# A hybrid decoder step on one core: weight sums of a seven-product matrix block done by accumulating transfers

## The reference

```python
a, b = split(rmsnorm(x) @ w_in, 2)
x = x + 0.5 * (silu(a) * b) @ w_out
```

## Time and profile before

| what | value |
|---|---|
| median of 3 runs | 2186.99 us (2185.7 to 2189.09) |
| the profiled execution | 2188.33 us, span 2186.6 us |
| mean granted TensorE clock | 0.995 of full speed |
| busy: PE, DVE, ACT, POOL | 98%, 73%, 41%, 0% of the span |
| the DMA queues: SP's, POOL's | 35.5%, 0.3% of 16 engines' span |
| chain of work that ended last | PE 93%, DVE 5%; seven-product blocks (L2631) 33% |

### The profile page before, as it was taken

One profiled execution on the slowest core, in us unless ns is written; L12 is line 12 of the kernel. 1 busy time (PEld: TensorE's weight loads), 2 busy tenths in 40 slices (PEclk: granted clock), 3 DMA queues, 4 the chain that ended last, 5 costly groups with the idle time before them and its releaser, 6 DMA issues.

```text
span 2186.6 us, 42987 instructions
## 1 busy us (share of the span) xinstructions
PE 2142.7 (98%) x17360; PEld 2108.6 (96%) x17360; DVE 1600.6 (73%) x2462; ACT 906.9 (41%) x1284; POOL 5.7 (0%) x19
## 2 busy tenths in 40 slices
PE   9999999999999989999999999999989999999998
PEld 8999999999999889999999999999988999999998
DVE  5766776457878789778487887848797579686774
ACT  5222232234545455445155543515533345253443
POOL 0000000000000000000000000000000000000000
PEclk9999999999999999999999999999999999999999
DMA  5233543243242144445245242424374434242332
GB/s 142 77 90 105 161 128 108 73 116 80 60 117 60 52 117 113 129 125 146 63 128 138 68 124 85 142 64 116 109 218 149 108 91 124 84 137 87 97 88 81
DMA packets 439814, 234.91 MB, mean 107 GB/s; under 512 B 34849, under 2 KB 432370, under 8 KB 439666
## 3 DMA queue, kind: packets, MB, share of 16 engines
q1 hardware_dynamic: 426562, 218.76, 35.5%
q10 hardware_dynamic: 12528, 13.08, 1.8%
q0 software_dynamic: 576, 1.05, 0.3%
HBM read 212.67 MB, written 23.30 MB: 108 GB/s over the span
## 4 chain that ended last, share of the span: by engine, by line
PE 93%; DVE 5%; issue 1%; DMA 1%; ACT 1%; SPq 0%; DVEq 0%; ACTq 0%
PE ps L2519 52%; PE ps L2631 33%; PE ps L2748 2%; PE ps L2482 1%; PE ps L2938 1%; PE ps L2927 1%; PE ps L2913 0%; PE ps L2826 0%; DVE w_lo L1500 0%; DVE o_rs L2243 0%; DMA w_raw<-in_ffn_w_in_dram 0%; DMA wb<-wb_d 0%; PE ps L2790 0%; PE ps L2799 0%; PE ps L2817 0%
## 5 line engine op out<-in xcount | busy, mean ns | idle before, releaser
L2631 PE MATMUL ps<-hf_hi,s_hi 128*128 128x288 f32 x1848 | 547.6, 296 | 9.6 <-issue 4.5
L2631 PE MATMUL ps<-hf_lo,s_hi 128*128 128x288 f32 x1848 | 543.2, 294 | 0.0
L2631 PE MATMUL ps<-hf_hi,s_lo 128*128 128x288 f32 x1848 | 542.5, 294 | 0.0
L2631 PEld LDWEIGHTS ps<-hf_hi,s_hi 128*128 128x128 f32 x1848 | 346.9, 188 | 12.6 <-issue 7.2
L2631 PEld LDWEIGHTS ps<-hf_lo,s_hi 128*128 128x128 f32 x1848 | 347.2, 188 | 0.2
L2631 PEld LDWEIGHTS ps<-hf_hi,s_lo 128*128 128x128 f32 x1848 | 346.9, 188 | 0.0
L1588 DVE TENSOR_TENSOR s_lo<-s_raw,s_hi 128x1024 fp32r<-128x1024 f32 (+1 forms) x264 | 286.5, 1089 | 60.6 <-ACT s_hi L987 52.9
L987 ACT ACTIVATE s_hi<-s_raw 128x1024 fp32r<-128x1024 f32 (+1 forms) x264 | 250.2, 950 | 191.5 <-PE ps L2631 183.2
L929 ACT ACTIVATE w_hi<-w_raw 128x1024 fp32r<-128x1024 f32 (+4 forms) x141 | 185.7, 1323 | 242.4 <-PE ps L2519 239.4
L2519 PE MATMUL ps<-h_hi,w_hi 128*128 128x288 f32 x1216 | 267.8, 302 | 2.2 <-issue 1.1
L2519 PE MATMUL ps<-h_hi,w_lo 128*128 128x288 f32 x1216 | 260.5, 296 | 0.0
(11 more groups left out here) (415 smaller groups left out, 3081.1 us busy)
## 6 DMA issues: line engine op xcount, KB each, us to landing
s_raw<-in_ffn_w_in_dram SPq DMA_DIRECT2D x330, 256.0 KB, 3.3
w_raw<-in_ffn_w_out_dram SPq DMA_DIRECT2D x96, 256.0 KB, 3.2
w_raw<-in_ffn_w_in_dram SPq DMA_DIRECT2D x44, 512.0 KB, 5.1
w_raw<-in_hgrn_w_in_dram SPq DMA_DIRECT2D x32, 512.0 KB, 5.4
w_raw<-in_ffn_w_out_dram SPq DMA_DIRECT2D x48, 192.0 KB, 2.6
w_raw<-in_s_w_glu_dram SPq DMA_DIRECT2D x16, 512.0 KB, 5.1
w_raw<-in_ffn_w_out_dram SPq DMA_DIRECT2D x16, 384.0 KB, 4.0
w_raw<-in_ffn_w_out_dram SPq DMA_DIRECT2D x16, 320.0 KB, 3.7
```

Source lines behind the costliest of these rows:

```text
L2631: ins = M.matmul(out, w, h, start=f in (0, 1, 3) and k == 0 and n == 0, stop=f in (3, 5, 6) and k == KP - 1 and n == 2, skip_group_check=True)
```

## The change

The set of pooled units grows from two to 56: units 4 to 21 of each of the three blocks are added, in order of v. For these, the first and second sum are accumulating transfers issued by POOL, and VectorE's two instructions go. As a semaphore now serves many units, the counts waited for grow by 32 for each pooled unit of the same parity.

```diff
-        POOLED = (UNITS, UNITS + 1)
+        POOLED = (UNITS, UNITS + 1) + tuple(q * UNITS + u for q in range(len(FAST)) for u in range(4, UNITS))
+        POOLED = tuple(sorted(POOLED))
+
+        def n_pooled(v):
+
+            return 32 * sum(p <= v and p % 2 == v % 2 for p in POOLED)
...
                 if v in POOLED:
-                    act.wait_ge(pool_sums[v % 2], 32)
+                    act.wait_ge(pool_sums[v % 2], n_pooled(v))
                 elif g == 0:
                     act.wait_ge(sum1_done[v % 2], n_sum(v))
...
                 if v in POOLED:
-                    dve.wait_ge(pool_sums[v % 2], 32)
+                    dve.wait_ge(pool_sums[v % 2], n_pooled(v))
                 else:
                     dve.wait_ge(a_ld[v % 2], 32 * (v // 2 + 1))
```

## The result

The changed kernel takes 2251.52 us (median of four runs, 2250.31 to 2254.88) against 2187.26 us for the kernel before in four runs beside it: a ratio of 1.0289, with an interval of 1.0272 to 1.0307. The direction was forecast; the size, 64 us, is nearly three times the forecast 22.7, and lies outside the range. The profiled execution has a span of 2248.4 us against 2186.6, so 61.8 us have to be found. Lines of the kernel have moved: the fifth piece's load is now L716 (L711 before), the two accumulating transfers L902 and L904, ScalarE's split L992, its copies L1039, VectorE's third sum L1576, the products L2636.

The account below looks back on a forecast made before the run. TensorE, busy 98% of the span, was taken to bound the kernel. Ordinary units' stalls of 10.6 us plus late ones' 12.1 gave +22.7 us on the median 2186.99, so 2210 us, range 2190 to 2236.

Parts of the forecast that it names:

- TensorE bound, VectorE's relief worth nothing: TensorE never pauses in a group of eight units; VectorE loses 108 sums, 73 us, and the critical path gains 0.
- The tight spot: ScalarE's first split now needs both sums; two PSUM copies queue behind it, and product 4 of unit v-1 waits for them.
- Slack 0.48, ordinary 0.4; the second sum 3.75: Before product 4: 0.48 us to spare, 0.4 at the median fifth-piece landing, with the second sum landing 3.75 us after issue.
- Lateness 0.75 of the fifth piece: The first sum's hold on the DMA engines makes the fifth piece's load, issued 1.1 us after it, land 0.75 us late.
- The two bounds: Fifth-piece lateness of 0.3 us from a piece issued 0.2 us after the first sum, 1.3 from one issued 0.7 after.
- What is given back: A stall before product 4 delays the fifth piece, not the first sum, so it settles at half the miss: 0.28 us.
- Late ones, 12.1 us: Ten of 48 transitions, mostly at group ends, with late fifth pieces: 4.6 us of excess plus 10 x 0.75, not halved.
- A third load late round the loop: The second sum delays the next unit's third load, starting its first sum 0.4 us later; lateness 0.75 becomes up to 1.15.
- Queue built up: Rival: transfers and loads jam the DMA engines, lateness 1.3 us, nothing given back: 52 us, 2239 us; chance 0.15.
- Shared turn by turn: Rival: DMA engines alternate between queues, fifth-piece lateness 0.35 us everywhere, only the ten late transitions pay: 2195 us; chance 0.12.
- Hidden: Rival: accumulates delay no fifth piece, which lands within 3.3 us in ordinary units: 2187 to 2191.6 us; chance 0.20.
- The two rules of the Trainium skill: DMA page: 2.6 us for a 256 KB GpSimd transfer, and engines alternating queues packet by packet; the forecast preferred the profile rows.

Follow-up runs that it names:

- every second unit: Changed kernel with only the 27 even ones of the 54 new units transferred, the odd ones summed on VectorE: 2219.77 us, 1.0145.
- the changed one without the edges: Changed kernel with each group's last unit (places 5, 13, 21 of a block) and unit 6 summed on VectorE again: 2225.61 us, 1.0173.
- the later first sum: Changed kernel with POOL issuing a new unit's first sum only when product 4 of unit v-2 is over: 2220.85 us, 1.0142.
- the kernel with copies: Changed kernel with the 108 new transfers as plain copies that add nothing, the sums left out: 2199.18 us, 1.0050.

## Why the direction was right and the size wrong

**TensorE bound, VectorE's relief worth nothing.** Right: 0.9993 with the sums left out. One detail was off: VectorE lost 60.3 us of busy time, not 73, since neighbouring instructions overlap (1116.20 + 0.69 against a next start at 1116.81), which the mean duration counts twice. It decides nothing.

**The tight spot.** Right: ScalarE's first split, the copies behind it, product 4. TensorE waits there in 25 places and the chain passes through it three times in the group shown. Moving the wait for the second sum took away some 39 us.

**Slack 0.48, ordinary 0.4; the second sum 3.75.** The slack holds: with the second sum alone, 38 transitions stay without a stall at 2.90 + 0.32 + 3.73 us. But 3.75 was taken from two landings, the second sums of units 22 and 23, with no load issued in the 1.2 us behind them, and kept unchanged. This is **the step that failed most**. With the fifth piece late, the second sum is issued late as well, beside the next unit's first loads, which SP issues when product 0 of unit v-1 is over. In the stalled transitions it then takes 4.88 us, 1.1 more. The ordinary units (those of the 48 away from the edges) of three kernels, the changed one, every second unit, and the changed one without the edges, show how sharp this is: where the next unit's first load is issued less than 0.5 us behind the second sum, or ahead of it, the sum takes 4.87 us on average (28 units), from 0.5 to 1.0 us behind it 4.45 (19), and later 3.75 (56). All of those 47 stall, and of the 56 only seven. The prediction had the second sum hold up the loads, and never asked what the loads do to the second sum. The DMA queues in the changed kernel, from 1112.8 to 1115.8, show it (last section): the packets of both share the engines. The trace of the kernel before had a sign of it: its two first sums, each with a fifth piece issued 0.2 or 0.7 us behind it, took 4.7 and 4.2 us.

```profile
DMA to landing us min/median/max: 4.2/4.5/4.7
```

**Lateness 0.75 of the fifth piece.** Right in kind, too small. The same ordinary units of the same three kernels, sorted by how long after the first sum the fifth piece was issued, with mean landings and stall in us:

```
issued after first sum   units   fifth piece   second sum   stall
before it                   14          3.12         3.89    0.14
0.00 to 0.25                11          3.25         3.75    0.04
0.25 to 0.50                12          4.25         4.70    2.37
0.50 to 0.75                 8          4.13         4.58    1.71
0.75 to 1.00                18          4.14         4.62    1.65
1.00 to 1.20                12          3.95         4.54    1.33
1.20 to 1.40                 8          3.65         4.10    0.51
1.40 to 1.70                 5          3.29         3.71    0.00
over 1.70                   15          2.90         3.50    0.00
```

A load issued together with the sum gets ahead of it, one issued a quarter of a microsecond later meets nearly the whole hold, and from there the lateness falls. So the reason given, that at 1.1 us less of the hold is left, holds, but there it is still 1.05 and not 0.75; "midway" between two units at 0.2 and 0.7 us mixed one that got ahead with one that met the hold. The two bounds lay on either side of an edge, not at the ends of a slope. In the changed kernel the 18 stalled transitions of ordinary units have an offset of 0.5 us on average and a lateness of 1.2, near the upper bound.

**What is given back.** Right in kind, wrong in the figure. A stall does delay the fifth piece and not the first sum, and a fifth piece issued 1.4 us or more after the sum goes free (the table). But it doesn't settle at half the miss: about half of the transitions (18 of 39) pay it whole and the others nothing. The whole miss of these 18, by their own landings of 4.09 and 4.67 us, is 1.2 + 0.9 - 0.4 = 1.7 us. Their waits average 1.6, their stalls 34.0 / 18 = 1.9: the rest is TensorE's lower clock behind some of the waits, for which the forecast had no term (last section). Per ordinary transition that is 0.9, where the forecast had 0.28.

**Late ones, 12.1 us.** Right in place for the most part, half the size: the forecast's ten have 23.6 us, in seven of them, and the nine edges 25.3. There the sums meet not only the next unit's loads but the output phase's weights; with the later first sum, holding those weights back took away the seven stalls that it reached. The term had only the fifth piece's excess and the same 0.75.

**A third load late round the loop.** It exists: at the first break above the third load took 3.81 us where the unit of the rows had 3.3, the first sum was issued so much later, and the offset is 0.65 us where the forecast had 1.1 for the unit that it followed (17, which here has 1.8 and no stall). But it isn't needed: with every second unit, 18 ordinary ones stall by 1.36 us on average with no pooled neighbour.

**The nearest rival.** *Queue built up* gave 2239, with a price per unit of 0.9 us, which is what came out by luck, through another mechanism than the queue it was named for. The range stopped at 2236, short of that rival's end; and with the second sum's lateness in the sum, neither price would have been an end. *Shared turn by turn* and *Hidden* are refuted by the landings.

**The two rules of the Trainium skill.** The rows were rightly preferred, but both rules are better than I used them. Its page "DMA: Bandwidth & Descriptors", section "Anatomy of one DMA", has 2.0 us plus bytes over 436 GB/s, an estimate of 2.6 us for 256 KB: the plain copies take 2.4 and agree, the accumulating ones 3.7 and don't. The same page, section "Queues, rings and completion order", has an engine drain a whole packet of some 9 to 17 descriptors from one queue before it turns to the next. I read that as fine alternation. The queue row of the changed kernel has 16128 entries for 112 transfers, 144 each, 9 for each of 16 engines: if these make one packet, a sum's whole share on an engine goes through before a load gets its turn, which is what the standstill of the earlier trace rows looks like. No run here shows where a packet of the page ends.

## What to carry to other kernels

Before work is moved to an idle queue, ask what else runs on the transfer engines in the microseconds in which it will move, and price both directions: what it does to the loads, and what the loads do to it. A chain load, transfer, wait has two landings in a row, and a lateness of the first shifts the second into other company. And ask first what the relieved engine's time is worth: here a kernel without the work would have said zero.

## What the runs showed of the hardware

**An accumulating transfer costs more than twice a plain one.** The changed kernel's 8.5% of 2248.4 us over 112 transfers is 1.7 us of all 16 engines for each. In the kernel with copies, 3.9% of 2196.4 is 85.7 us; less four sums at 1.7, the 108 copies take 0.73 us each. Issuing one takes POOL 0.86 us against 0.54.

**Whoever comes first holds the engines.** The DMA queues in the changed kernel (packets, MB, share of the 16 engines), first behind the first sum of 1106.27, from 1107.5 to 1109.5, then around the second sum of 1111.37, from 1112.8 to 1115.8:

```profile
q0 software_dynamic: 117, 0.24, 87.2%
q1 hardware_dynamic: 153, 0.07, 14.6%
...
q0 software_dynamic: 144, 0.26, 52.9%
q1 hardware_dynamic: 618, 0.31, 37.2%
```

In the first stretch the sum holds the engines and the loads get 0.07 MB through. In the second, the next unit's loads, though issued 0.33 us after the sum, have their packets first (from 1112.73 on), and the sum's begin at 1113.90, 2.5 us after its issue; the first sum's began 1.4 us after its own.

**A stall can cost clock as well.** After TensorE's longest wait its products begin every 0.24 us in place of 0.13, and the granted clock of the stretch (the first of the last three columns of the second view: PEclk, DMA share, GB/s) is 0.89:

```profile
904.21 0.58 PE L2636 MATMUL ps<-hf_hi,s_hi 128*128 128x288 f32 x1 [4.93 <-ACT fau L1039]
904.59 0.44 PE L2636 MATMUL ps<-hf_lo,s_hi 128*128 128x288 f32 x1
904.83 0.44 PE L2636 MATMUL ps<-hf_hi,s_lo 128*128 128x288 f32 x1
```

```profile
896.00:912.00 16.00, 11.07 (x73) 10.86 (x73) 7.75 (x11) 6.15 (x9) 2.58 (x3) 0.89 0.65 156
```

This is the lower of the two levels, 1.2 GHz. It came seven times behind the waits of the changed kernel, for 3.4 us each, always beginning within 1.6 us of the end of a wait of 2.0 to 5.1 us; other waits of 1.9 to 3.0 us went without. With 12 to 15 products each that are some 0.11 us late, it makes about 10 us of the 59.4 above, and the mean granted clock falls from 0.995 to 0.989. A stall that is priced by the idle time alone comes out too small.
